# The entry stage of a hybrid decoder layer: first weights in four transfers, two modulation rows in one PSUM bank, their sums inside a projection chunk

## What is computed

```python
mod = jax.nn.silu(c) @ w_ada + b_ada
shift1, scale1, gate1, shift2, scale2, gate2 = jnp.split(mod, N_MOD, axis=-1)
h = _modulate(_rms_norm(x, norm1_g), shift1, scale1)   # h*(1+scale1)+shift1
proj = h @ w_in
...                                                    # retention heads, sparse attention heads
x = x + gate1[:, None, :] * mix
h = _modulate(_rms_norm(x, norm2_g), shift2, scale2)
y = jnp.square(jax.nn.relu(h @ w_mlp1)) @ w_mlp2
return x + gate2[:, None, :] * y
```

## Time and profile before

| what | value |
|---|---|
| median of 3 runs | 2438.81 us (2431.74, 2438.81, 2439.72) |
| the profiled execution, its own time | 2437.39 us |
| its span in the trace | 2435.6 us |
| mean granted TensorE clock | 0.987 |
| TensorE busy | 2374.5 us, 97% |
| VectorE busy | 990.3 us, 41% |
| ScalarE, GpSimd busy | 640.1 us, 973.3 us |
| HBM traffic | 342.89 MB, 141 GB/s over the span |

### The profile page before, as it was taken

One profiled execution on the slowest core, in us unless ns is written; L12 is line 12 of the kernel. 1 busy time (PEld: TensorE's weight loads), 2 busy tenths in 40 slices (PEclk: granted clock), 3 DMA queues, 4 the chain that ended last, 5 costly groups with the idle time before them and its releaser, 6 DMA issues.

```text
span 2435.6 us, 26802 instructions
## 1 busy us (share of the span) xinstructions
PE 2374.5 (97%) x10878; PEld 1926.7 (79%) x10878; DVE 990.3 (41%) x1365; ACT 640.1 (26%) x894; POOL 973.3 (40%) x414
## 2 busy tenths in 40 slices
PE   6999998999999999899999999999999999999999
PEld 4687687788878887788888888888888888888887
DVE  2237899877744777732022031131121221221121
ACT  4222332223223221232122232222221221221232
POOL 1233243234433334354444444444444444444442
PEclk8999999999999999999999999999999999999999
DMA  9975465667833532222333223322323223322331
GB/s 355 347 277 198 149 214 191 211 226 271 289 109 104 207 122 83 91 90 83 104 104 101 81 96 104 105 95 79 105 104 101 80 97 104 105 88 85 104 125 49
DMA packets 183695, 342.89 MB, mean 141 GB/s; under 512 B 4337, under 2 KB 31124, under 8 KB 182804
## 3 DMA queue, kind: packets, MB, share of 16 engines
q1 hardware_dynamic: 174944, 336.77, 40.4%
q10 hardware_dynamic: 8628, 4.28, 0.6%
HBM read 324.26 MB, written 16.78 MB: 140 GB/s over the span
## 4 chain that ended last, share of the span: by engine, by line
PE 87%; DVE 8%; DMA 3%; issue 1%; ACT 1%; SPq 0%; POOL 0%; ACTq 0%; DVEq 0%
PE pj L1189 51%; PE pa L1189 30%; DVE part_rows L1008 1%; DVE score L933 1%; DVE m L932 1%; DMA ada_first<-w_ada_in 1%; PE pa L1193 1%; PE pa L1261 1%; DVE sq L1165 1%; PE pa L1380 1%; DMA raw<-w_in_in 1%; DVE ada_acc L1008 1%; DMA resid<-xT_dram 1%; PE pa L1414 1%; PE pa L1437 1%
## 5 line engine op out<-in xcount | busy, mean ns | idle before, releaser
L733 POOL TENSOR_TENSOR w_lo<-raw,w_hi 128x1024 fp32r<-128x1024 f32 (+1 forms) x396 | 954.8, 2413 | 1400.1 <-ACT w_hi L501 1400.1
L501 ACT ACTIVATE w_hi<-raw 128x1024 fp32r<-128x1024 f32 (+1 forms) x396 | 416.1, 1054 | 1533.4 <-PE pj L1189 993.0
L1189 PE MATMUL pj<-h,w_hi 128*128 128x512 f32 x1664 | 520.9, 394 | 4.0 <-DVE h L828 2.5
L1189 PE MATMUL pj<-w_hi,h 128*128 128x512 f32 (+1 forms) x1536 | 482.1, 391 | 16.1 <-DVE rot L960 9.6
L1189 PEld LDWEIGHTS pj<-h,w_hi 128*128 128x128 f32 x1664 | 312.3, 190 | 76.3 <-issue 11.2
L1165 DVE TENSOR_TENSOR sq<-relu 128x512 f32<-128x512 f32 x64 | 160.5, 2508 | 517.0 <-ACT relu L689 517.0
L1189 PEld LDWEIGHTS pj<-w_hi,h 128*128 128x128 f32 x1536 | 287.6, 190 | 88.2 <-issue 24.8
L1189 PE MATMUL pa<-h,w_hi 128*128 128x512 f32 x1152 | 357.2, 391 | 0.0
L1189 PE MATMUL pj<-h,w_lo 128*128 128x512 f32 x832 | 326.0, 392 | 0.0
L1189 PE MATMUL pj<-mid,w_hi 128*128 128x512 f32 x1024 | 316.7, 390 | 5.6 <-DVE mid L1169 5.6
L1189 PE MATMUL pa<-mid,w_hi 128*128 128x512 f32 x1024 | 316.0, 390 | 0.0
(11 more groups left out here) (167 smaller groups left out, 1690.9 us busy)
## 6 DMA issues: line engine op xcount, KB each, us to landing
raw<-w_mlp_in SPq DMA_DIRECT2D x64, 2048.0 KB, 8.8
ada_rows<-w_ada_in SPq DMA_DIRECT2D x64, 1024.0 KB, 5.1
raw<-w_in_in SPq DMA_DIRECT2D x22, 2048.0 KB, 10.1
ada_first<-w_ada_in SPq DMA_DIRECT2D x32, 1024.0 KB, 9.8
raw<-w_out_in SPq DMA_DIRECT2D x8, 2048.0 KB, 8.0
ret<-ret_dram SPq DMA_DIRECT2D x32, 256.0 KB, 3.8
raw<-w_in_in SPq DMA_DIRECT2D x4, 1792.0 KB, 14.6
x_nat<-x_in SPq DMA_DIRECT2D x4, 1024.0 KB, 9.7
```

Source lines behind the costliest of these rows:

```text
L501: act.activation(split_chunk(w_hi, u, j), raw_chunk(u, j), ACT.Copy).then_inc(hi_done, 1)
L733: pool.tensor_tensor(split_chunk(w_lo, u, j), raw_chunk(u, j), split_chunk(w_hi, u, j).bitcast(F32), ALU.subtract).then_inc(lo_done, 1)
L1189: last = pe.matmul(dst, lhs[a], rhs[b], start=start and n == 0, stop=stop and n == 2)
```

## The change

1. Unit 0 is fetched in four transfers, one for each chunk (`load_quarter`, own semaphores). The first goes ahead of group 0's piece 6, the other three behind piece 7. ACT splits each quarter as it lands; it makes the first split before it copies the row bank, and the other three each after one HI slice of h.
2. Scale and shift rows share one accumulation in bank 3. c_wide is one long row of columns with silu(c) at column 1 of every 32; a scale piece takes the 32 columns from offset 1, a shift piece those from offset 0, so silu(c) stands in column 0 or 1 of the stationary operand, and the shift row comes out one partition below the scale row. All 32 matmuls of a group accumulate into one bank; ACT copies it once. `pick` (128 x 2, built by DVE from the identity) is the moving operand of the sums: four matmuls with two columns in place of eight with one.
3. `sum_first(cc)` for cc = 1 to 3 stands inside the chunk of place 3, behind its products for tb = 0 and 1, instead of ahead of the chunk.
4. Behind the sums of group 0, seven matmuls of 128 x 128 of the identity with itself go into pj, whose result is overwritten.

c_wide, rstd1 and shift_part move or go; the first split's wait for raw_landed changes its count, since unit 0 no longer uses that semaphore.

```diff
+            def load_quarter(j):
+                sp.dma_start(raw[:, 0, EARLY * j:EARLY * j + EARLY], unit_source(0)[:, j, :]).then_inc(quarter_landed[j], 16)
...
             for t in range(4, 8):
+                if t == 6:
+                    load_quarter(0)
                 first_piece(0, t)
-            load_unit(0)
+            for j in range(1, 4):
+                load_quarter(j)
...
-            def take_first(cc, sec):
-                act.wait_ge(first_used, 8 * cc + 4 * sec + 4)
+            def take_first(cc):
+                act.wait_ge(first_used, 8 * cc + 8)
                 need(act, mod_summed, cc)
-                act.activation((shift_part if sec else part_rows)[:], pa[:, 3, :], ACT.Copy).then_inc(first_taken, 1)
+                act.activation(part_rows[:], pa[:, 3, :], ACT.Copy).then_inc(first_taken, 1)
...
             for cc in range(4):
-                if cc == 0:
-                    take_first(0, 1)
                 for j in range(4):
-                    if cc > 0 and j % 2 == 0:
-                        take_first(cc, j // 2)
+                    if cc > 0 and j == 2:
+                        take_first(cc)
                     split_hi(cc, j)
+                    if cc == 0:
+                        if j == 0:
+                            take_first(0)
+                        h_high(j)
                     if cc > 0 and j == 2:
                         for m in range(4):
                             h_high(4 * cc + m)
-                if cc == 0:
-                    for m in range(4):
-                        h_high(m)
...
-            def silu_rows(src, s, start, stop):
+            def silu_rows(src, s, sec):
                 for i in range(4):
-                    last = pe.matmul(pa[32 * i:32 * i + 32, 3, :], c_wide[:, 4 * s + i, :], src[i], start=start, stop=stop)
+                    at_ = 32 * (4 * s + i) + 1 - sec
+                    last = pe.matmul(pa[32 * i:32 * i + 32, 3, :], c_wide[:, at_:at_ + 32], src[i],
+                                     start=sec == 0 and s == 0, stop=sec == 1 and s == 3)
...
             def sum_first(cc):
-                pe.wait_ge(first_taken, 2 * cc + 2)
-                for sec, part in enumerate((part_rows, shift_part)):
-                    for m in range(4):
-                        last = pe.matmul(pa[:, 3, 4 * sec + m:4 * sec + m + 1], part[:, P * m:P * m + P], ones[:, 0:1],
-                                         start=True, stop=True)
+                pe.wait_ge(first_taken, cc + 1)
+                if cc == 0:
+                    pe.wait_ge(c_wide_ready, 2)
+                for m in range(4):
+                    last = pe.matmul(pa[:, 3, 2 * m:2 * m + 2], part_rows[:, P * m:P * m + P], pick[:],
+                                     start=True, stop=True)
                 last.then_inc(mod_summed, 1)
...
-            def early_chunk(kt):
+            def early_chunk(kt, group):
...
+                    if tb == 1 and group is not None:
+                        sum_first(group)
...
             pe.wait_ge(x_taken, 16)
+            for _ in range(7):
+                pe.matmul(pj[:, 0, 0:P], ident, ident, start=True, stop=True)
```

More of the change, by code:

```diff
@@ L167, in build @@
     q_gain = small("q_gain", 8)
+    pick = small("pick", 2)
     RC = RB + 4352 + 2048
@@ L182, in build @@
     ikT = at("ikT", RC + 30720, [P, L])
-    rstd1 = at("rstd1", RC + 32768, [P, L])
+    rstd1 = at("rstd1", RC + 34816, [P, L])
     x_junk = at("x_junk", RC + 12288, [P, D])
@@ L187, in build @@
     junk = at("junk", RC + 34816, [P, L])
-    shift_part = at("shift_part", RC + 34816, [P, L])
-    c_wide = at("c_wide", RC + 2048, [P, KT, 32])
+    c_wide = at("c_wide", RC + 30720, [P, KT * 32 + 32])
     stage = at("stage", RC + 36864, [P, 2, L])
@@ L226, in build @@
     raw_landed = [sem("raw_landed0"), sem("raw_landed1")]
+    quarter_landed = [sem(f"quarter_landed{j}") for j in range(4)]
     xT_stored, resid_landed = sem("xT_stored"), sem("resid_landed")
@@ L498, in split_hi @@
                 need(act, chunk_used, 4 * (u - 1) + j + 1 + 4 * PER_C * trip)
-                if j == 0:
-                    act.wait_ge(raw_landed[u % 2], 16 * (u // 2 + 1) + 16 * (PER_C // 2) * trip)
+                if u == 0:
+                    act.wait_ge(quarter_landed[j], 16)
+                elif j == 0:
+                    act.wait_ge(raw_landed[u % 2], 16 * ((u + 1) // 2) + 16 * (PER_C // 2) * trip)
                 act.activation(split_chunk(w_hi, u, j), raw_chunk(u, j), ACT.Copy).then_inc(hi_done, 1)
-            def take_first(cc, sec):
-                act.wait_ge(first_used, 8 * cc + 4 * sec + 4)
+            def take_first(cc):
+                act.wait_ge(first_used, 8 * cc + 8)
                 need(act, mod_summed, cc)
-                act.activation((shift_part if sec else part_rows)[:], pa[:, 3, :], ACT.Copy).then_inc(first_taken, 1)
+                act.activation(part_rows[:], pa[:, 3, :], ACT.Copy).then_inc(first_taken, 1)
             def h_high(kt):
@@ L646, in _ @@
                     act.activation(csilu[:, 1, :], vec[:, V_C:V_C + KT], ACT.Exp, scale=-1.0).then_inc(silu_exp, 1)
-                if tb == 2:
-                    take_first(0, 0)
                 act.wait_ge(x_landed[tb % 2], 16 * (tb // 2 + 1))
@@ L790, in _ @@
             own.wait()
-            dve.tensor_copy(c_wide[:, :, 0], csilu[:, 0, :]).then_inc(c_wide_ready, 1)
+            dve.tensor_copy(c_wide[:, 1:1 + KT * 32].rearrange("p (k a) -> p k a", a=32)[:, :, 0],
+                            csilu[:, 0, :]).then_inc(c_wide_ready, 1)
+            own.link(dve.tensor_tensor(pick[:], ident[:, 0:2], ident[:, 32:34], ALU.add))
+            own.link(dve.tensor_tensor(pick[:], pick[:], ident[:, 64:66], ALU.add))
+            dve.tensor_tensor(pick[:], pick[:], ident[:, 96:98], ALU.add).then_inc(c_wide_ready, 1)
             def take_mod(n):
@@ L802, in take_first_mods @@
                 dve.wait_ge(mod_summed, cc + 1)
+                sums_ = pa[:, 3, 0:8].rearrange("p (m sec) -> p sec m", sec=2)
                 for sec in range(2):
                     col = KT * (1 - sec) + 4 * cc
-                    dve.tensor_tensor(mod[:, col:col + 4], pa[:, 3, 4 * sec:4 * sec + 4], bias_cols[:, col:col + 4],
+                    dve.tensor_tensor(mod[:, col:col + 4], sums_[:, sec, :], bias_cols[:, col:col + 4],
                                       ALU.add).then_inc(mod_taken, 1)
@@ L1269, in first_rows @@
                     pe.wait_ge(c_wide_ready, 1)
[L1270 to L1275, removed]
-            def sum_first(cc):
-                pe.wait_ge(first_taken, 2 * cc + 2)
-                for sec, part in enumerate((part_rows, shift_part)):
-                    for m in range(4):
-                        last = pe.matmul(pa[:, 3, 4 * sec + m:4 * sec + m + 1], part[:, P * m:P * m + P], ones[:, 0:1],
-                                         start=True, stop=True)
+                if t == 0:
+                    need(pe, first_taken, cc)
+                    need(pe, mod_taken, 2 * cc)
+                silu_rows([first[t % 4][:, 512 * i:512 * i + 512] for i in range(4)], s, sec).then_inc(first_used, 1)
+            def sum_first(cc):
+                pe.wait_ge(first_taken, cc + 1)
[4 more added lines that the diff above has]
+                                     start=True, stop=True)
                 last.then_inc(mod_summed, 1)
-            def early_chunk(kt):
+            def early_chunk(kt, group):
                 j = kt % 4
@@ L1322, in _ @@
                             first_rows(cc, t)
-                        if s == 3:
-                            sum_first(cc)
-                    early_chunk(4 * (cc - 1) + s)
+                    early_chunk(4 * (cc - 1) + s, cc if cc < 4 and s == 3 else None)
             for j in range(4):
```

## The result

| | median us | runs | lowest to highest |
|---|---|---|---|
| before | 2433.55 | 9 | 2429.47 to 2440.54 |
| changed | 2423.07 | 9 | 2422.14 to 2426.10 |

What follows compares the result with a forecast made beforehand. The prediction took TensorE, busy 97% of the span, as the bound, with the entry stage as the exception holding idle time. Gains of 3.1 + 4.2 + 1.6 = 8.9 us off 2437.39 gave 2428.5 us, range 2424.5 to 2435.5.

Steps and rivals of the forecast that it cites:

- Start of chunk 0: Entry stage: chunk 0 starts at 45.0 to 46.6 us instead of 49.01, 2.4 to 4.0 us earlier.
- What transfers leave: Entry stage, group 1: chunk 2 waits for piece 5 and starts at 64.15 instead of 67.27, a gain of 3.1 us.
- Sums in the chunk: Groups 1 to 3: sums issued inside the chunk save 1.4 us a group, 4.2 us for three.
- Clock at group 3: Chunk 8 to chunk 12: the fall of TensorE's granted clock goes away, worth 1.6 us.
- The basis: Whole kernel: the gain was counted from the profiled execution, 2437.39 us, not from the median of three runs.
- The clock in the new wait: Rival, between chunks 1 and 2: the clock falls and chunk 2 pays 2.8 us, giving 2431.3; chance 0.16.
- Each transfer pays its own start: Rival, entry-stage loads: three added transfers put group 1 back by 6.6 us, giving 2435.1; chance 0.08.
- Given back downstream: Rival, 300 to 700 us: TensorE's wait for VectorE grows, half the gain is lost, giving 2432.9; chance 0.12.
- Slower by the pieces: Rival, entry-stage groups: pieces become the pace and every wait drops the clock, +12.5 us, giving 2449.9; chance 0.04.

Runs made afterwards that it cites:

- e2: The changed kernel run again with nothing changed: 2424.71 us, ratio 0.9946 to the kernel before of its session.
- e3: The changed kernel without the seven filler identity products: 2424.65 us, ratio 0.9951 to the kernel before.
- e4: The changed kernel with unit 0 in one transfer behind piece 7, as before: 2424.77 us, ratio 0.9944 to the kernel before.
- e9: The changed kernel with the four sums of groups 1 to 3 again ahead of the chunk: 2425.16 us, ratio 0.9954 to the kernel before.
- e5: The kernel before with nine one-column matmuls added at TensorE's start: 2443.6 us, ratio 1.0022 to the kernel before.
- e11: The kernel before with the load of resid split into two transfers: 2435.13 us, ratio 0.9992 to the kernel before.
- e1: The kernel before run again with nothing changed, for a second profile: 2437.4 us, ratio 1.0004.
- e13: The changed kernel with the sums of groups 1 to 3 ahead of their chunk, each done twice: 2432.01 us, ratio 0.9979 to the kernel before.
- e6: The changed kernel with nine one-column matmuls added at TensorE's start: 2424.82 us, ratio 0.9946 to the kernel before.

## Why the prediction fell short, step by step

*Start of chunk 0.* Forecast 45.0 to 46.6, measured 47.13 (46.02 in e2). The clock was at half rate over pieces 6 and 7 (1.94 and 1.88 us instead of 1.06), and piece 7's products ended at 42.4, not 40.4. The slice was as quick as forecast: bias add 44.32 to chunk 0 at 47.13 is 2.8 us.

*What transfers leave.* Right, and the step on which most hung: chunk 2 at 64.15 forecast, 64.54 measured, 2.7 of 3.1 us. Fillers and quarters worth nothing: right (e3, e4).

*Sums in the chunk.* Forecast 1.4 us a group, measured 1.4 for the first (4.16 at chunk 4 less the 2.73 above) and 29.62 - 28.47 = 1.15 for the other two: 3.7 of 4.2. But the reason was half wrong. I gave the gain to the place; e9 with the sums ahead has 28.72, so the place is worth 0.25 and the halved number of sums 0.9. The wait for h ahead of chunks 4, 8 and 12 is 0.15, as forecast (0.2).

*Clock at group 3.* **This step failed: the term was too small.** In the profiled pair it is exact: 2.7 + 3.7 + 1.6, 8.1 us before rounding, at chunk 12. But "so I take the fall away: 1.6 us" took the one fall of one execution for a property of the kernel. The kernel before has one to three (8 of 12 groups in four profiles: two of itself, and e5 and e11, whose edits lie elsewhere), each worth 1.6 us, and the change takes away all of them. It also sometimes has a later chunk 0 (51.65 in e5, 53.53 in e1), in good part from VectorE's slower tiles; the changed kernel was not seen to have that (47.13 and 46.02 in its two profiles). The last y_raw is 7.7 us later than in the changed kernel with one fall and 15.5 later in e1 with three. That spread shows in the times too: 11 us between the lowest and the highest of before, 4 of the changed kernel. The mean granted clock of the timed executions goes with it: 0.983 to 0.991 in twenty of the kernel before, 0.989 to 0.990 in the fourteen of the changed one.

*The basis.* **This failed too, and in the result it is the larger part.** The sum was taken from one execution, 2437.39, and put at nothing whatever the change does behind the entry stage. That execution holds some 6 us for resid, which the changed kernel doesn't spend, and I had no row on it. Against the profiled pair, then, what failed is this silent zero: the spans differ by 14.3 us, of which the entry stage explains 7.7 and the stretch behind the last y_raw 6.6. Against the medians it is the basis: 2433.55 in place of 2437.39 makes 3.8 of the 5.4 us of miss. In the session of e2 the kernel before stood at 2436.29, and there the larger part, 2.7 of 3.8 us, is gain that I hadn't counted. An estimate of that gain: if 8 falls in 12 groups mean two an execution, the saving is the 8.1 of the pair, 1.6 us for the second fall, and from the resid wait 1.8 (e11's difference of medians, with an interval down to nothing). That makes 9.7 to 11.5, where 10.5 and 11.6 were measured. It is a weak proof, since the intervals of the measured ratios are some 6 us wide and the four profiles aren't typical: e1's and e5's are the slowest of their runs, e11's is among the fastest. How the remainder divides between more falls, late chunk 0 and resid is open.

*The rivals.* The clock in the new wait: no, it is 1.00 over 61 to 66 us. Each transfer pays its own start: no, piece 5 landed at 63.43 and e4 is equal. The Trainium skill ("DMA: Bandwidth & Descriptors", the section on the anatomy of one DMA) has its fixed cost of some 2 us per DMA from transfers issued by GpSimd; here, issued by SyncE into a queue that is kept full, it isn't paid in series. Given back downstream: no, the wait of TensorE for VectorE between 300 and 700 us is 8.2 us here and 9.6 in e2, against the 9.4 of the earlier trace rows:

```profile
PE pj L1201 <- DVE rot L972: 8.2, 6, 4.7
```

Slower by the pieces: no, a period takes 28.47 us and has no wait for a piece, though its rate of 341 to 351 GB/s is under the 362 at which I had this rival begin. Such a window moves 9.7 to 10.0 MB, not the 10.2 that I gave a group.

## What to carry to other kernels

A clock fall that one profile shows once in three like places is a chance, not a count: profile a second execution before pricing it, and price the change as what it does to the chance in every such place. Take the basis of a forecast from the median of many runs, and ask what the profiled execution holds that the others may not. In this kernel, where a wait of 0.72 us stood ahead of 16 thin passes, halving them or putting full products on either side both kept the clock; one of the two was enough. And when many small gains stand ahead of one transfer, only its landing counts.

## What was unexpected of the hardware

- The granted clock fell to 1.2 GHz in a period in which TensorE was busy 30.51 of 31.23 us, with one wait of 0.72 us ahead of 16 thin passes (e13), and didn't with the same wait ahead of 8 (e9). The Trainium skill ("TensorE: Matmul & The Clock Gate", the sections on oscillation and on depth-cycling) tells of falls behind waits for a transfer between tiles, and of falls from frequent short idles between groups of matmuls. The trace of e13 has neither around its falls, but one short wait with thin passes behind it.
- DMA issues of SyncE took longer where an instruction fetch of 16 KB fell on them: the four ret loads took 3.39, 3.23, 2.99 and 2.59 us in the four profiles with a fetch in their time (before, e1, e6, e11), and 2.01 us in the thirteen without. The Trainium skill ("Runtime: NRT & Kernel Launch", instruction fetch mechanics) has blocks of 16 KiB, which the one packet of 0.02 MB agrees with, and calls their cost mostly hidden; here 0.6 to 1.4 us of issue time went with one fetch. Whether fetches are also behind e5's five waits of about 1 us for "issue" in a loop, with nine tiny matmuls added far ahead of it, isn't shown.
